# An expert's two vectors fetched by two indirect transfers instead of one

## The chip, the cores and the metric

The kernel runs on one core of one Trainium2 chip. The metric is the device time of one execution in microseconds (us). A core has TensorE (PE, matmuls), VectorE (DVE), ScalarE (ACT), GpSimd (POOL) and SyncE (SP), which run their own instruction streams and meet at semaphores, and 16 DMA engines that all queues share. SP and ACT issue plain transfers; GpSimd issues the indirect ones, which fetch rows named by indices in on-chip memory.

## The reference, cut to what matters

Two transformer blocks over 256 tokens of width 1024, in fp32. The second block has two layers, and each ends in a layer of "product key" experts: every token picks, for each of 8 heads, 16 of 16,384 experts, each a pair of vectors `u` and `v` of 1024 numbers.

```python
def peer_ffn(x, w_q, sub_keys, u, v):
    ...
        top_s, pos = lax.top_k(cand_s, PEER_TOPK)
        eidx = jnp.take_along_axis(cand_i, pos, axis=-1)
        gate = jax.nn.softmax(top_s, axis=-1).astype(xb.dtype)
        h = jax.nn.gelu(jnp.einsum('thkd,td->thk', u[eidx], xb), approximate=False)
        return jnp.einsum('thk,thkd->td', gate * h, v[eidx])
```

So for 2 layers x 256 tokens x 8 heads x 16 experts, two rows of 4 KB must be read: 536.9 MB in all. `u` is needed for a dot product with the token; `v` only afterwards, when the weight `gate * h` is known.

## The kernel before

The work of a layer's experts is cut in 16 units (2 groups of 128 tokens x 8 heads), each of 16 slots. A slot is one expert for each of 128 tokens, one token per partition. There are 256 slots per layer, 512 in all. The fetched vectors lie in `G`, a ring of `RING` = 8 slots with 2 x 1024 fp32 per partition. The first 1024 columns hold `u` and the last 1024 hold `v`, because the host has laid the two tables side by side (`uv0`, `uv1`: rows of 8 KB). A slot goes through five steps, each on its own engine:

1. GpSimd (L801 to L815) waits for `slot_free`, for the first slot of a unit also for `idx_ready`, and issues one indirect transfer of 128 rows of 8 KB into the slot, by the indices in a column of `EIDX`. It signals `gathered[slot]`. In the tables of the trace this is `arena<-uv,expert_index`.
2. VectorE (`slot_dots`, L1481 to L1486) waits for `gathered` and makes the dot product of `u` with the token.
3. ACT (`slot_weights`, L1015 to L1024) makes a diagonal matrix from gelu of the dot product (L1020), times the gate (L1023), and signals `diag_ready`.
4. TensorE (`weigh_slot`, L640 to L647) waits for `diag_ready` and multiplies the diagonal with `v`, in two matmuls of 512 columns that add up in PSUM over all slots. In the profile each is two records.
5. The second matmul signals `slot_free`, which lets GpSimd fill the slot again.

Beside the dot products VectorE picks the next units' experts: `piece` cuts the top-16 search of a unit into 16 pieces, one after each slot's dot product. TensorE, during the first 128 tokens of a layer, computes later heads' queries between the slots (`query_step`, L655) from weights that SP's queue streams in blocks of 1 MB (`w_ring`, L362). During the second 128 tokens no weights come. At the end of the first 128 tokens' work, their output norm (`output_norm`) runs on VectorE in the midst of the last unit, after its ninth slot. Then come the norm of the other tokens and the next layer; at the very end the output is stored by SP (L373), 128 rows of 4 KB for each group of tokens.

Of the kernel before, what the change touches and what calls it, by code (L numbers as in the profile page):

```python
# [176 lines left out]
        c.leave(times)  # L177


def build(nc, stream, keys, cols, rows, x_cm, p_cm, sgu_wt, rcnt_in, positions, decay, uv0, uv1, out):  # L180
    ctx = ExitStack()
    with ctx:
        def sb(name, shape, dt=FP32):
# [2 lines left out]
        def sem(name):  # L186
            return ctx.enter_context(nc.semaphore(name))
# [149 lines left out]
        idx_ready = sem("idx_ready")  # L337
        top_ready = sem("top_ready")
        exp_ready = sem("exp_ready")
        gathered = [sem(f"gathered{i}") for i in range(RING)]  # L340
        slot_free = sem("slot_free")
        dots_ready, gates_ready, diag_ready = sem("dots_ready"), sem("gates_ready"), sem("diag_ready")
        experts_summed = sem("experts_summed")
# [34 lines left out]
        def _(pe):  # L378
# [258 lines left out]
                ring.wait_stored(ring.n - 1)  # L637
                key_scores(2)

            def weigh_slot(tt, s, count):  # L640

                pe.wait_ge(diag_ready, count)
                slot = s % RING
                for c in range(2):
                    last = nc.tensor.matmul(AUX[2 * tt + c][:, :], DG[:, slot, :],  # L645
                                            G[:, slot, D + c * 512:D + (c + 1) * 512], start=False, stop=False)
                last.then_inc(slot_free, 1)  # L647

            def query_step(s):

# [16 lines left out]
            def experts(layer):  # L667
                base = layer * (PEER_SLOTS + 1) + 1
                for u in range(HEADS):
                    for s in range(TOPK):  # L670
                        weigh_slot(0, s, base + u * TOPK + s + 1)
                        if 1 <= u <= HEADS - AHEAD and s == 2:

                            ring.wait_stored(ring.n - 1)
                            key_scores(u + AHEAD - 1)
                        if u < HEADS - AHEAD:

                            for k in range(3) if u and s == 2 else () if u and s < 2 else (s,):
                                query_step(k)
                end_tokens(0)  # L680
                with pe.Fori(0, HEADS) as i:
                    for s in range(TOPK):
                        weigh_slot(1, s, base + HEADS * TOPK + s + 1 + i * TOPK)
                end_tokens(1)

            peer(0)
# [71 lines left out]
        @block.gpsimd  # L758
        def _(pool):
            chain = Chain(pool, pool_chain)  # L760
            link = chain.link
            nc.gpsimd.memset(ONES[:, :], 1.0).then_inc(ones_ready, 1)
            nc.gpsimd.memset(PADH[:, :, 0:PAD], 0.0)
            nc.gpsimd.memset(PADZ[:, :, 0:ZPAD], 0.0).then_inc(pads_ready, 1)
            link(nc.gpsimd.memset(IDENT[:, :], 1.0))
            link(nc.gpsimd.affine_select(out=IDENT[:, :], in_=IDENT[:, :], pattern=[[-1, P]],
                                         compare_op=ALU.is_equal, fill=0.0, base=0, channel_multiplier=1))
            nc.gpsimd.memset(ZERO[:, :], 0.0)
            link(nc.gpsimd.memset(ALPHA_I[:, :], ALPHA))
            nc.gpsimd.affine_select(out=ALPHA_I[:, :], in_=ALPHA_I[:, :], pattern=[[-1, P]],  # L770
                                    compare_op=ALU.is_equal, fill=0.0, base=0,
                                    channel_multiplier=1).then_inc(ident_ready, 1)
            link(nc.gpsimd.iota(IOTAI[:, :], pattern=[[1, TOPK]], base=0, channel_multiplier=0))
            link(nc.gpsimd.tensor_copy(IOTA16[:, :], IOTAI[:, :]))
            pool.sem_inc(iota_ready, 1)

            pool.wait_ge(sgu_w_loaded, 16)
            link(nc.gpsimd.memset(WS[P // 2:P, :, 0:P // 2], 0.0))
            pool.sem_inc(sgu_w_ready, 1)

            pool.wait_ge(small_loaded, 16)
            for u in range(8, 12):
                pool.wait_ge(acc_free[u % BANKS], u // BANKS + 1)
            for g in range(len(WINDOWS)):
                src, lo = PADZ[:, 2 * g:2 * g + 2, :], 0
                for n in range(g + 1):
                    dst, step = (PA, PB)[n % 2], 2 ** n
                    lo += step
                    link(nc.gpsimd.tensor_tensor(dst[:, :, lo:ZPAD + S], src[:, :, lo:ZPAD + S],
                                                 src[:, :, lo - step:ZPAD + S - step], ALU.add))  # L790
                    src = dst
                link(nc.gpsimd.tensor_tensor(POOLED[:, 2 * g:2 * g + 2, :], src[:, :, ZPAD:ZPAD + S],
                                             RC[:, g:g + 1, :].broadcast_to([P, 2, S]), ALU.mult))
                last = nc.gpsimd.tensor_tensor(POOLED[:, 2 * g:2 * g + 2, :], POOLED[:, 2 * g:2 * g + 2, :],
                                               PADZ[:, 2 * g:2 * g + 2, ZPAD:ZPAD + S], ALU.subtract)
                link(last) if g < 3 else last.then_inc(pooled_ready, 1)

            pool.wait_ge(input_ready, 10)
            nc.gpsimd.iota(DIFI, pattern=[[-P, 2], [1, S]], base=0, channel_multiplier=-1).then_inc(iota_ready, 1)  # L799

            for layer in range(2):  # L801
                uv = (uv0, uv1)[layer]
                free0 = layer * (RING + PEER_SLOTS)
                with pool.Fori(0, UNITS // 2) as i:
                    for par in range(2):
                        for s in range(TOPK):
                            n = par * TOPK + s
                            pool.wait_ge(slot_free, free0 + n + 1 + i * 2 * TOPK)
                            if s == 0:
                                pool.wait_ge(idx_ready, layer * UNITS + par + 1 + i * 2)  # L810
                            pool.sem_inc(waits_passed, 1)
                            pool.indirect_dma_start(  # L812
                                G[:, s % RING, :], None, uv,
                                bass.IndirectOffsetOnAxis(ap=EIDX[:, par, s:s + 1], axis=0),
                            ).then_inc(gathered[s % RING], 16)  # L815


        @block.scalar
# [285 lines left out]
        def _(dve):  # L1104
# [279 lines left out]
            def peer(layer):  # L1384
# [96 lines left out]
                def slot_dots(tt, unit, s, i):  # L1481
                    slot, n = s % RING, n0 + unit * TOPK + s
                    landed = 16 * (n // RING + 1)
                    dve.wait_ge(gathered[slot], landed if i is None else landed + i * 16 * (2 * TOPK // RING))
                    v.scalar_tensor_tensor(G[:, slot, 0:D], G[:, slot, 0:D], 1.0, HTM[:, tt, :], ALU.mult, ALU.mult,  # L1485
                                           accum_out=HD[:, slot:slot + 1]).then_inc(dots_ready, 1)  # L1486

# [123 lines left out]
def _layout(inputs):  # L1611
# [68 lines left out]
    def cm(a):  # L1680
# [8 lines left out]
        "sgu_wt": f("w_sgu_s")[0].transpose(2, 0, 1),  # L1689
        "rcnt": np.stack([1.0 / np.minimum(t1, np.float32(w)) for w in WINDOWS]).astype(np.float32),  # L1690
        "positions": f("positions_2")[0], "decay": f("ret_log1m_decay_2")[0].reshape(-1),
        "uv0": np.concatenate([f("peer_u_2")[0], f("peer_v_2")[0]], axis=1),
        "uv1": np.concatenate([f("peer_u_2")[1], f("peer_v_2")[1]], axis=1),
    }


# [12 lines left out]
```

## Time and profile before

| | |
|---|---|
| time, median of 3 runs | 2521.17 us (2519.57 to 2522.03) |
| the profiled execution | 2519.95 us, its span 2518.0 us |
| TensorE busy | 2187.0 us, 87% |
| VectorE busy | 1204.9 us, 48% |
| ACT busy | 687.8 us, 27% |
| GpSimd busy | 587.4 us, 23% |
| DMA | 701.47 MB, 279 GB/s over the span |
| of it the software queue (GpSimd's) | 536.90 MB, 51.3% of the engines' time |

The span is the time from the first to the last instruction of the profiled execution. Busy shares are means over the whole span, in which stages with different limits follow each other. The page therefore also cuts the span in 40 slices of 63 us, with each engine's busy tenths and the rate of the DMA engines in each. A "share of 16 engines" for a DMA queue is the sum of the times that its packets took, over 16 times the stretch asked for; packets may overlap a little, so it can exceed 100%.

### The profile page before, as it was taken

The numbers are of one execution on the slowest core, as the hardware profiler recorded it, in microseconds if no ns is written. First come the engines' busy times: TensorE is split into PE (matmuls) and PEld (weight loads), VectorE is DVE, ScalarE is ACT, GpSimd is POOL, SyncE is SP. The second block draws the span as 40 slices with busy tenths as digits, with TensorE's granted clock in tenths as the row PEclk, the third lists the DMA queues.
The fourth block names the chain that finished last, engine by engine and source line by source line (L and its number), as shares of the span: only waits on it lengthen the run. The fifth ranks groups of instructions, "written<-read, shape, count | busy, mean of one in ns | idle before, by whom it ended". The sixth has DMA issues, their size and how long they took to land.

```text
span 2518.0 us, 23594 instructions
## 1 busy us (share of the span) xinstructions
PE 2187.0 (87%) x7202; PEld 1339.6 (53%) x7202; DVE 1204.9 (48%) x2852; ACT 687.8 (27%) x1472; POOL 587.4 (23%) x546
## 2 busy tenths in 40 slices
PE   7989998999999997999878777778788997878786
PEld 6858887888775785444322222256654442322222
DVE  3972112000240204666666766522256666666665
ACT  1001101000201103343434344322234343434433
POOL 0300000000000001344444444400023444444441
PEclk9999998999999998999999999989999999999998
DMA  5433432444343234999999999921179999999997
GB/s 216 151 117 137 148 142 100 154 144 145 134 150 134 100 134 194 421 421 422 422 422 421 422 422 422 422 91 67 69 313 421 422 422 421 422 421 422 422 422 292
DMA packets 96981, 701.47 MB, mean 279 GB/s; under 512 B 10896, under 2 KB 11152, under 8 KB 11792
## 3 DMA queue, kind: packets, MB, share of 16 engines
q0 software_dynamic: 73728, 536.90, 51.3%
q1 hardware_dynamic: 21600, 156.25, 17.3%
q10 hardware_dynamic: 1584, 7.41, 0.8%
q8 instruction: 42, 0.69, 0.1%
q14 instruction: 27, 0.22, 0.0%
HBM read 699.47 MB, written 1.05 MB: 278 GB/s over the span
## 4 chain that ended last, share of the span: by engine, by line
PE 47%; DMA 34%; issue 7%; DVE 6%; ACT 4%; DVEq 1%; POOL 0%; POOLq 0%; ACTq 0%
DMA arena<-uv,expert_index 34%; PE acc L407 31%; PE aux L645 8%; PE acc L435 2%; DVE arena L1170 2%; PE aux L469 1%; ACT arena L1020 1%; ACT arena L1023 1%; DVE arena L1485 1%; PE acc L655 1%; PE aux L488 1%; DVE rstd L1124 0%; PE acc L599 0%; DVEq L106 0%; PE aux L634 0%
## 5 line engine op out<-in xcount | busy, mean ns | idle before, releaser
L645 PE MATMUL aux<-arena 128*128 128x512 f32 x2048 | 1015.2, 625 | 215.9 <-ACT arena L1023 210.2
L812 POOL DMA_INDIRECT arena<-uv,expert_index x512 | 561.7, 1097 | 1238.5 <-PE aux L645 670.5
L1485 DVE SCALAR_TENSOR_TENSOR arena<-arena 128x1024 f32<-128x1024 f32 x512 | 635.1, 1241 | 439.5 <-DMA arena<-uv,expert_index 439.5
L645 PEld LDWEIGHTS aux<-arena 128*128 128x128 f32 x2048 | 364.3, 193 | 791.8 <-ACT arena L1023 506.3
L407 PE MATMUL acc<-x,w_ring 128*128 128x256 f32 x2544 | 564.5, 385 | 27.7 <-issue 12.3
L407 PEld LDWEIGHTS acc<-x,w_ring 128*128 128x128 f32 x2544 | 491.2, 193 | 100.5 <-issue 23.5
L1020 ACT ACTIVATE arena<-ident,dots 128x128 f32<-128x128 f32 x512 | 205.3, 401 | 740.9 <-DVE arena L1485 739.3
L407 PE MATMUL acc<-arena,w_ring 128*128 128x256 f32 x1416 | 312.8, 383 | 13.5 <-DVEq L1551 7.0
L407 PEld LDWEIGHTS acc<-arena,w_ring 128*128 128x128 f32 x1416 | 271.1, 192 | 53.4 <-DVEq L1551 7.4
L1023 ACT ACTIVATE arena<-arena,gate 128x128 f32<-128x128 f32 x512 | 205.4, 401 | 17.0
L799 POOL IOTA arena<- 128x512 int32 x1 | 0.6, 558 | 556.4 <-DVEq L1281 556.4
L1170 DVE SCALAR_TENSOR_TENSOR arena<-arena,channel_vectors x240 | 112.2, 548 | 0.2 <-DVE arena L1170 0.2
L833 ACT ACTIVATE arena<-acc 128x512 f32<-128x512 f32 (+1 forms) x65 | 38.5, 595 | 250.2 <-PE acc L407 248.1
L655 PEld LDWEIGHTS acc<-x,w_ring 128*128 128x128 f32 x320 | 60.8, 192 | 67.0 <-issue 66.2
L655 PE MATMUL acc<-x,w_ring 128*128 128x256 f32 x320 | 93.5, 382 | 0.0
L435 PE MATMUL acc<-w_ring,x 128*128 128x512 f32 x192 | 82.7, 592 | 0.0
L1262 DVE TENSOR_TENSOR arena<-acc,arena 128x256 f32 x20 | 8.5, 425 | 131.7 <-ACT arena L921 131.7
L435 PEld LDWEIGHTS acc<-w_ring,x 128*128 128x128 f32 x192 | 36.5, 190 | 45.1 <-issue 45.0
L911 ACT ACTIVATE scratch<-arena 128x512 f32<-128x512 f32 x8 | 5.0, 629 | 189.2 <-DVE arena L1238 189.2
L1238 DVE COPY arena<-acc 128x512 f32<-128x512 f32 x8 | 5.5, 692 | 103.9 <-PE acc L407 103.9
L1129 DVE TENSOR_SCALAR rstd<-aux 128x256 f32<-128x256 f32 x9 | 3.8, 425 | 95.9 <-PE aux L469 92.1
L469 PE MATMUL aux<-scratch,ones 128*128 128x256 f32 x90 | 28.7, 488 | 22.3 <-ACT scratch L850 12.4
(209 smaller groups left out, 1079.4 us busy)
## 6 DMA issues: line engine op xcount, KB each, us to landing
w_ring<-stream SPq DMA_DIRECT2D x147, 1024.0 KB, 4.7
arena<-uv,expert_index POOLq DMA_INDIRECT x512, 14.9
x<-keys ACTq DMA_DIRECT2D x2, 1024.0 KB, 4.7
row_vectors<-rows ACTq DMA_DIRECT2D x2, 1024.0 KB, 8.1
row_vectors<-rows ACTq DMA_DIRECT2D x1, 1536.0 KB, 11.8
x<-x_cm SPq DMA_DIRECT2D x1, 1024.0 KB, 5.6
out<-arena SPq DMA_DIRECT2D x2, 512.0 KB, 5.1
arena<-rcnt ACTq DMA_DIRECT2D x1, 512.0 KB, 15.3
```

Source lines behind the costliest of these rows:

```text
L407: last = nc.tensor.matmul(ring.bank()[:, half * S:(half + 1) * S], w[:, 0, :], x[:, k, :], start=(k == 0), stop=(k == kt - 1))
L435: last = nc.tensor.matmul(bank[:, :], x[:, k, tt * P:(tt + 1) * P], w, start=(k == 0), stop=(k == kt - 1))
L469: last = nc.tensor.matmul(AUX[3 - half][:, 0:S], ONES[:, :], x[:, k, :], start=(k == 0), stop=(k == kt - 1))
L488: last = nc.tensor.matmul(AUX[3][:, 0:S], ONES[:, :], src[:, k, :], start=(k == 0), stop=(k == KT - 1))
L645: last = nc.tensor.matmul(AUX[2 * tt + c][:, :], DG[:, slot, :], G[:, slot, D + c * 512:D + (c + 1) * 512], start=False, stop=False)
L655: last = nc.tensor.matmul(ring.bank()[:, half * S:(half + 1) * S], w[:, 0, :], X0[:, k, :], start=(k == 0), stop=(k == KT - 1))
L812: pool.indirect_dma_start(G[:, s % RING, :], None, uv, bass.IndirectOffsetOnAxis(ap=EIDX[:, par, s:s + 1], axis=0),).then_inc(gathered[s % ...
L833: ring.release(nc.scalar.activation(dst, halves(ring.bank()), func, scale=scale))
L1020: link(nc.scalar.activation(DG[:, slot, :], IDENT[:, :], ACT.Gelu, scale=HD[:, slot:slot + 1]))
L1023: nc.scalar.activation(DG[:, slot, :], DG[:, slot, :], ACT.Copy, scale=GT[:, par, s:s + 1]).then_inc(diag_ready, 1)
L1170: chain.step(v.scalar_tensor_tensor(CV[:, j + c, :], at, w, CV[:, j + c, :], ALU.mult, ALU.add))
L1485: v.scalar_tensor_tensor(G[:, slot, 0:D], G[:, slot, 0:D], 1.0, HTM[:, tt, :], ALU.mult, ALU.mult, accum_out=HD[:, slot:slot + 1]).then_in ...
```

## The change

Each slot gets two indirect transfers, each of 128 rows of 4 KB. The first brings `u` into the slot's first half and signals `down_landed[slot]`, the second brings `v` into its second half and signals `up_landed[slot]`. The tables are four arrays instead of two. VectorE waits for the first signal alone. TensorE gets a wait for the second, ahead of the one for `diag_ready`. GpSimd's waits stay once per slot. The ring, the order of slots and the computation stay as they are.

```diff
-        gathered = [sem(f"gathered{i}") for i in range(RING)]
+
+        down_landed = [sem(f"down_landed{i}") for i in range(RING)]
+        up_landed = [sem(f"up_landed{i}") for i in range(RING)]
...
-            def weigh_slot(tt, s, count):
-
+            def weigh_slot(tt, s, count, landed):
+
+                pe.wait_ge(up_landed[s % RING], landed)
                 pe.wait_ge(diag_ready, count)
...
+            def landed(layer, unit, s):
+
+                return 16 * ((layer * PEER_SLOTS + unit * TOPK + s) // RING + 1)
...
-                uv = (uv0, uv1)[layer]
+                downs, ups = ((u0, v0), (u1, v1))[layer]
...
                             pool.indirect_dma_start(
-                                G[:, s % RING, :], None, uv,
+                                G[:, s % RING, 0:D], None, downs,
                                 bass.IndirectOffsetOnAxis(ap=EIDX[:, par, s:s + 1], axis=0),
-                            ).then_inc(gathered[s % RING], 16)
+                            ).then_inc(down_landed[s % RING], 16)
+                            pool.indirect_dma_start(
+                                G[:, s % RING, D:2 * D], None, ups,
+                                bass.IndirectOffsetOnAxis(ap=EIDX[:, par, s:s + 1], axis=0),
+                            ).then_inc(up_landed[s % RING], 16)
...
-                    dve.wait_ge(gathered[slot], landed if i is None else landed + i * 16 * (2 * TOPK // RING))
+                    dve.wait_ge(down_landed[slot], landed if i is None else landed + i * 16 * (2 * TOPK // RING))
...
-        "uv0": np.concatenate([f("peer_u_2")[0], f("peer_v_2")[0]], axis=1),
-        "uv1": np.concatenate([f("peer_u_2")[1], f("peer_v_2")[1]], axis=1),
+        "u0": f("peer_u_2")[0], "v0": f("peer_v_2")[0], "u1": f("peer_u_2")[1], "v1": f("peer_v_2")[1],
```

## Rows read from the trace of the kernel before

**Rows 1.** The page, the span in 40 slices: busy tenths, and GB/s of the DMA.

```profile
PE   7989998999999997999878777778788997878786
DVE  3972112000240204666666766522256666666665
POOL 0300000000000001344444444400023444444441
DMA  5433432444343234999999999921179999999997
GB/s 216 151 117 137 148 142 100 154 144 145 134 150 134 100 134 194 421 421 422 422 422 421 422 422 422 422 91 67 69 313 421 422 422 421 422 421 422 422 422 292
```

**Rows 2.** The page, the chain that ended last, shares of the span by engine.

```profile
PE 47%; DMA 34%; issue 7%; DVE 6%; ACT 4%; DVEq 1%; POOL 0%; POOLq 0%; ACTq 0%
```

**Rows 3.** DMA view, 1400 to 1500 us: packets, and the software queue (packets, MB, share).

```profile
DMA packets 5794, 42.21 MB, mean 422 GB/s; under 512 B 642, under 2 KB 642, under 8 KB 642
...
q0 software_dynamic: 5794, 42.21, 101.4%
```

**Rows 4.** The gather's line, L812, over the span.

```profile
L812 POOL DMA_INDIRECT arena<-uv,expert_index x512: 935/939/1994, 985.7 to 2484.6; - x171
...
DMA to landing us min/median/max: 5.6/14.9/19.4
```

**Rows 5.** Timeline, 1501 to 1514 us: start, us, engine, line, operation, [idle before].

```profile
1501.00 0.94 POOL L812 DMA_INDIRECT arena<-uv,expert_index  x1 [1.55 <-PE aux L645]
1501.01 1.25 DVE L1485 SCALAR_TENSOR_TENSOR arena<-arena 128x1024 f32<-128x1024 f32 x1 [1.00 <-DMA arena<-uv,expert_index]
...
1502.30 0.40 ACT L1020 ACTIVATE arena<-ident,dots 128x128 f32<-128x128 f32 x1 [1.65 <-DVE arena L1485]
1502.73 0.40 ACT L1023 ACTIVATE arena<-arena,gate 128x128 f32<-128x128 f32 x1
...
1503.19 1.98 PE L645 MATMUL aux<-arena 128*128 128x512 f32 x4 [0.50 <-ACT arena L1023]
...
1510.95 1.23 DVE L1485 SCALAR_TENSOR_TENSOR arena<-arena 128x1024 f32<-128x1024 f32 x1 [0.69 <-DMA arena<-uv,expert_index]
1511.04 1.96 POOL L812 DMA_INDIRECT arena<-uv,expert_index  x1 [1.62 <-PE aux L645]
```

**Rows 6.** DMA view, 2506 to 2518 us: the last store, alone on the engines.

```profile
DMA packets 144, 0.52 MB, mean 44 GB/s; under 512 B 16, under 2 KB 16, under 8 KB 144
...
q1 hardware_dynamic: 144, 0.52, 10.8%
...
out<-arena SPq DMA_DIRECT2D x1, 512.0 KB, 2.6
```

**Rows 7.** DMA view, 1700 to 1712 us: a weight load, SP's queue.

```profile
q1 hardware_dynamic: 144, 1.05, 25.4%
```

**Rows 8.** The page, DMA issues: operation, count, KB each, median us to landing.

```profile
w_ring<-stream SPq DMA_DIRECT2D x147, 1024.0 KB, 4.7
```

**Rows 9.** Timeline, 985 to 990 us: GpSimd's first issues, and SP's of weights.

```profile
987.11 0.33 SPq L362 DMA_DIRECT2D w_ring<-stream  x1
987.19 0.94 POOL L812 DMA_INDIRECT arena<-uv,expert_index  x1 [0.30 <-issue]
...
988.44 0.94 POOL L812 DMA_INDIRECT arena<-uv,expert_index  x1 [0.30 <-issue]
```

**Rows 10.** Timeline of GpSimd, 112 to 140 us: two instructions, a wait between.

```profile
111.30 1.33 POOL L792 TENSOR_TENSOR arena<-arena 128x512 f32<-128x512 f32 x1
112.71 1.33 POOL L794 TENSOR_TENSOR arena<-arena 128x512 f32<-128x512 f32 x1
```

**Rows 11.** The page, costliest groups: busy us, mean ns, idle before by releaser.

```profile
L812 POOL DMA_INDIRECT arena<-uv,expert_index x512 | 561.7, 1097 | 1238.5 <-PE aux L645 670.5
L1485 DVE SCALAR_TENSOR_TENSOR arena<-arena 128x1024 f32<-128x1024 f32 x512 | 635.1, 1241 | 439.5 <-DMA arena<-uv,expert_index 439.5
```

**Rows 12.** Timeline, 2487 to 2508 us: VectorE's norm of the first tokens, TensorE's last slots.

```profile
2488.86 1.22 DVE L1516 TENSOR_TENSOR arena<-arena,row_vectors 128x1024 f32<-128x1024 f32 x1
...
2492.16 14.78 PE L645 MATMUL aux<-arena 128*128 128x512 f32 x28 [5.83 <-ACT arena L1023]
```

**Rows 13.** DMA view, weights' queue: 987 to 1320 us, and 1848 to 2180 us.

```profile
q1 hardware_dynamic: 864, 6.29, 4.5%
...
q1 hardware_dynamic: 432, 3.15, 2.3%
```

More of the change, by code:

```diff
@@ L177, in repeat, with build @@
         c.leave(times)
-def build(nc, stream, keys, cols, rows, x_cm, p_cm, sgu_wt, rcnt_in, positions, decay, uv0, uv1, out):
+def build(nc, stream, keys, cols, rows, x_cm, p_cm, sgu_wt, rcnt_in, positions, decay, u0, v0, u1, v1, out):
     ctx = ExitStack()
@@ L670, in experts @@
                     for s in range(TOPK):
-                        weigh_slot(0, s, base + u * TOPK + s + 1)
+                        weigh_slot(0, s, base + u * TOPK + s + 1, landed(layer, u, s))
                         if 1 <= u <= HEADS - AHEAD and s == 2:
@@ L682, in experts @@
                     for s in range(TOPK):
-                        weigh_slot(1, s, base + HEADS * TOPK + s + 1 + i * TOPK)
+                        weigh_slot(1, s, base + HEADS * TOPK + s + 1 + i * TOPK,
+                                   landed(layer, HEADS, s) + i * 16 * (TOPK // RING))
                 end_tokens(1)
@@ L1706 @@
     build(nc, ap["stream"], ap["keys"], ap["cols"], ap["rows"], ap["x_cm"], ap["p_cm"], ap["sgu_wt"], ap["rcnt"],
-          ap["positions"], ap["decay"], ap["uv0"], ap["uv1"], out)
+          ap["positions"], ap["decay"], ap["u0"], ap["v0"], ap["u1"], ap["v1"], out)
     return run(nc, [arrays], core_ids=[0]).results[0]["out"]
```

## The prediction

> **What bounds the kernel now.** I read the page's slices first. In the two stretches where the experts are gathered (slices 17 to 26 and 31 to 39) the 16 DMA engines are busy 9 tenths or more of the time and move 421 to 422 GB/s in nearly every slice, while TensorE, VectorE and GpSimd have slack [rows 1]. Outside them no gather runs, so the change can act only inside. The chain of waits puts 34% of the span on one transfer, `arena<-uv,expert_index` [rows 2]. Next the queue by itself, in 100 us without other traffic: 5794 packets, of which 144 make a transfer (128 rows of 8 KB, and 16 small ones that signal), so 40.24 transfers in 100 us: a period of 2.485 us for one expert slot of 128 tokens, at a busy share of 101.4% [rows 3]. The reader is to see that a share of 100% with a flat rate is a full pipe. The issues confirm it: median 14.9 us from issue to landing, minimum 5.6 [rows 4], so 9 us of queue stand in front of each gather. The ring of 8 slots closes the loop: 8 x 2.485 = 19.9 us, of which 14.9 are queue and transfer and 5.0 are dot product, diagonal, matmul and re-issue. From this I take it that a shorter reaction by any compute engine buys nothing there; only a cheaper or dearer transfer does, or an issuer that can't keep up.
>
> One slot in the timeline shows the other engines: dot product 1.25 us, ACT 0.40 + 0.40, matmuls 1.98, all inside the period of 2.49 [rows 5].
>
> **The change, part by part.**
>
> *DMA.* 512 gathers of 128 x 8 KB become 1024 of 128 x 4 KB: the same bytes, twice the packets. Now a slot takes 101.4% x 16 x 100 us / 40.24 = 40.3 us of engine time [rows 3]. The trace has no 4 KB gather. It has one transfer of that form alone on the engines, the last store, 128 rows of 4 KB: 144 packets, 10.8% of 16 x 12 us = 20.7 us [rows 6]. Two make 41.5 us, 1.029 times 40.3. The period grows to 2.485 x 1.029 = 2.556 us, +0.071; times 512 slots that is **+36.4 us**. Nothing hides it, because the engines are full [rows 1]. Bounds: below, nothing, since a lone weight load of 1 MB, also 8 KB rows, needed 25.4% x 16 x 12 = 48.8 us [rows 7], more than the two stores together, so packet size is not the only thing that prices a transfer. Above, by landing times: a 4 KB-row transfer lands after 2.6 us, an 8 KB-row one after 4.7 us [rows 6, 8]; two of the first cost 0.5 us more than one of the second, and were this shown in full, 512 slots would pay 256 us. But it is latency, and 9 us of queue lie over latency; I take +36, from the row that measures occupancy.
>
> The rows show 2.9% more for half the packet size, if a store stands for a gather. The Trainium skill (DMA: Bandwidth & Descriptors, Why small descriptors are slow) gives a fixed overhead of about 3 cycles a packet beside one cycle per 32 bytes; as an estimate from that page 262 cycles replace 259, 1.2%, and the sum would be about +15 us instead of +36. No row here separates the two.
>
> *GpSimd.* It issues twice per slot. An issue takes 0.94 us when nothing is in its way, and with all slots free the next follows 0.30 us later [rows 9]. The gap holds a wait and a counter, which the second issue of a slot lacks; two plain GpSimd instructions with a wait between them stand 0.08 us apart [rows 10]. So two issues cost 2 x 0.94 + 0.30 + (0.08 to 0.30) = 2.26 to 2.48 us, against 2.556 of DMA: just covered, by 0.08 to 0.30 us. Now the same engine has 1.24 us of work in 2.485 and nobody waits for it.
> There is a catch in the rows. When an issue begins inside a dot product on VectorE, it takes longer: begun 0.09 us after the dot product, it took 1.96 us and ended 0.8 us after the dot product's end; begun with it, 0.94 [rows 5]. The mean over 512 issues is 1.097 us [rows 11], 0.157 above the median of 0.939. Now most issues are released by TensorE at a point of the cycle just ahead of the dot product. With two per slot they can't both be there. I take the case that one waits for the dot product's end and the second fits behind it: 2.556 - 1.25 = 1.3 us are free of the dot product in each period, and two issue starts need 1.02 to 1.24 us between them. Then GpSimd follows the DMA's pace and costs nothing.
> The Trainium skill (SBUF — State Buffer, Who interferes with whom) says that a VectorE instruction with two SBUF inputs contends with a GpSimd instruction that reads SBUF, and that the later one waits; the 1.96 us row agrees. It speaks against this change, and the second and third case below are what it would do.
>
> *VectorE* waits for the first half alone, about 1.28 us sooner. Under a full queue that only moves its idle time: the 439.5 us of waiting [rows 11] are a wait for bytes. *TensorE* gets one wait more per slot, on the second half. That half lands about 1.28 us after the first, while the diagonal is ready only 1.25 + 0.1 + 0.85 = 2.2 us after it [rows 5]: satisfied 0.9 us before TensorE looks. Behind it in TensorE's queue stand the next slot's matmuls and query steps, and GpSimd waits for their release; if the cover were gone, the ring's queue time would still take up to 9 us. The instruction itself lies in TensorE's gap of 0.5 us per slot [rows 5]. *The ends*: at each layer's end TensorE works off a backlog of seven slots (28 matmuls in 14.8 us), since VectorE has spent the time before on the other tokens' norm [rows 12], so the earlier half saves between 0 and 1.28 us, twice; I take 0. *SP and ACT queues* keep their transfers; their 8 KB packets now stand beside 4 KB ones, which can only bring weights sooner. Tables in HBM keep their total size.
>
> **Sum.** 2519.95 us for the profiled execution (2518.0 span, 1.95 around it) + 36.4 = 2556.4. The median of the runs is 1.2 us above that execution: **2558 us**.
>
> **The rivals.**
>
> *GpSimd paces, one wait per slot* (chance 0.24). Gap 0.30 for both issues and the mean excess once per slot: 2 x 1.24 + 0.157 = 2.64 us per slot. It doesn't hold everywhere: in the first tokens' half of each layer weights share the engines, 4.5% of 333 us = 15.0 us in the first layer, 2.3% of 332 us = 7.6 in the second [rows 13]. Per half of 128 slots GpSimd needs 337.9 us, DMA 128 x 2.556 = 327.2 plus weights. Layer 1's first half is then DMA's, +9.1 us; layer 2's first half 337.9 - (318.1 + 7.6) = +12.2; the two second halves 337.9 - 318.1 = +19.8 each. Sum +60.9: 2582 us. For it: the gap of 0.30 is the only one measured between issues. Against: weights and jitter let it catch up.
>
> *GpSimd and VectorE in lock step* (0.12). Without a queue a half lands about 5.6 - 1.24 = 4.4 us after its issue, its dot product ends at 5.6, and the issue two slots later, due at 2 x 2.48 = 4.96, waits for that end: two slots per 5.6 us, 2.8 each. The mean issue gives nearly the same, 2 x (1.097 + 0.30) = 2.79. By halves as before: +24.5, +31.9 and twice +39.5, in all +135: 2656 us. For it: the start, where issues at 1.24 us and halves at 1.28 us build no queue. Against: a weight load of 2.5 us pushes the halves back and builds one, and one stands at 987.11, at the start of the gathers [rows 9].
>
> *Not slower* (0.08). Halves cost the engines no more per byte, which [rows 7] permit, and GpSimd keeps up; then the period stays 2.485 and the ends save up to 2 x 1.28: 2519 us. It decides where a slot's extra falls below 5.0 / 512 = 0.01 us. To be faster by over 0.2% it would need a rate above the flat 422 GB/s as well.
>
> *Forecast: the DMA engines pace* (0.50), own range 2539 to 2575: half to one and a half times the +36. *Something beyond these* (0.06): sixteen transfers in flight instead of eight, which no row shows, stop the issuer: above 2660.
>
> **Numbers.** This kernel's measurement tells about 0.2%, 5 us. Slower: 0.92 (the forecast, both GpSimd cases, the last). Within: 0.05, faster 0.03, both from the third rival. The range goes from 2539, below which only the third rival lies, to 2660, which takes in the lock step.
>
> **What the profile after would show.** Packets of the software queue double to 147,456 with the same bytes. If I am right, the gather stretches keep a busy share near 100% at about 410 GB/s (421 x 2.485 / 2.556), both halves of a layer grow alike (+9.1 us each), VectorE still waits for DMA, and GpSimd's issues number 1024 with idle time between them that TensorE ends. If GpSimd paces, the share falls to 95% or less in the second halves, landing times drop from 14.9 towards 5 us, GpSimd's idle time is "issue" alone, and its mean issue is over 1.1 us. What would make the forecast wrong first is the gap between a slot's two issues, then the share of issues that meet a dot product, then the price of a 4 KB read.

## The result and the profile after

The changed kernel takes 2720.45 us (median of 4 runs, 2714.16 to 2729.37), the kernel before took 2520.72 beside it: ratio 1.0795, interval [1.0759, 1.0831], about +200 us. The forecast was 2558, the range ended at 2660. The profiled execution took 2724.96 us with a span of 2723.1.

From the page after: DMA busy share and GB/s in 40 slices, the software queue, the chain by engine, and the three groups that answer to [rows 2, 11].

```profile
DMA  5433424443432369999999999621599999999997
GB/s 215 145 118 139 141 107 146 149 152 134 146 139 93 124 251 370 379 369 376 341 369 354 351 364 367 239 94 62 202 367 353 341 350 358 368 359 361 355 355 300
q0 software_dynamic: 147456, 536.94, 52.7%
PE 49%; issue 22%; POOL 10%; DMA 7%; DVE 5%; ACT 3%; another core or an unknown queue 3%; DVEq 1%; POOLq 0%; ACTq 0%
L1497 DVE SCALAR_TENSOR_TENSOR arena<-arena 128x1024 f32<-128x1024 f32 x512 | 627.0, 1226 | 617.0 <-DMA arena<-u,expert_index 544.7
L824 POOL DMA_INDIRECT arena<-v,expert_index x512 | 584.0, 1141 | 157.6 <-issue 150.2
L820 POOL DMA_INDIRECT arena<-u,expert_index x512 | 523.3, 1022 | 752.1 <-DVE expert_index L1480 505.1
```

Packets doubled at the same bytes, as the change says. But where before moved a flat 421 to 422 GB/s [rows 1], after moves 341 to 379, uneven from slice to slice, and the gather fell from 34% of the chain [rows 2] to 7%. DMA engines still read 9 tenths: the digit alone would hide the loss, the rate shows it. The engines are no longer a full pipe.

Where the time went: from the start of a layer's first issue to the end of its last, the gathers run from 987.05 to 1737.8 and from 1942.5 to 2703.7 us (before: 985.7 to 1629.6 and 1849.3 to 2485.6). Divided by 256 slots, a slot takes 2.93 and 2.97 us; before it took 2.515 and 2.486. That is +106.9 and +124.9 us. The stretch from the first layer's last issue to the second layer's first shrank by 15.0 us (219.7 to 204.7) and that from the last issue to the span's end by 13.0 (32.4 to 19.4), presumably because no queue is left to drain; the start is 1.4 later. In all +205.2, the difference of the spans (205.1).

GpSimd by itself explains 2.76 us of the 2.95: 1.022 and 1.141 us for the two issues, and twice a gap of 0.30 us. The remaining 0.18 us per slot are pauses: 35 gaps between issues exceed 1 us, and what they have over 0.30 us comes to 93 us in all; the longest are 4.4 us and, once, 10.5. Next the waits between 1000 and 1700 us, within layer 1's gathers, after: us in total, times, longest.

```profile
PEld aux L648 <- issue: 335.6, 639, 10.8
DVE arena L1497 <- DMA arena<-u,expert_index: 261.0, 198, 4.6
ACT arena L1032 <- issue: 231.8, 121, 5.7
ACT arena L1032 <- DVE arena L1497: 180.4, 87, 4.9
...
POOL arena L820 <- PE aux L648: 28.9, 16, 4.4
...
DVE top_pairs L1448 <- remote: 1.5, 1, 1.5
```

and the same view of the kernel before, 1000 to 1600 us, three of its eleven rows:

```profile
ACT arena L1020 <- DVE arena L1485: 343.6, 208, 4.1
POOL arena L812 <- PE aux L645: 325.6, 191, 5.8
...
PEld aux L645 <- issue: 127.0, 510, 0.5
```

Two things are new. Engines are idle for up to 10.8 us with the releaser "issue", that is, with nothing in the profile left to wait for; before, the longest such wait was 0.5 us at the same line. And VectorE waits for signals of its own chain (briefly here, the last row of the first table; for 2.17 us in a timeline below).

So the signals can be timed directly, by pairing each producer's end with its consumer's start and counting only the time in which the consumer had nothing else to do. For the activation on ACT that waits for the k-th dot product, that is its start, less the dot product's end or the end of ACT's operation before it, whichever is later. Before, none of the 512 starts is over 0.3 us late by this count; after, 16 are, the latest by 6.3 us. For GpSimd, it is the start of a slot's first issue, less the end of the matmul that frees the slot or the end of GpSimd's instruction before, over the 466 slots that wait for neither new indices nor the first fill of the ring. Before, 4 starts come over 1 us late; after, 30, the latest by 4.4 us. What those over 0.5 us have above the usual gap of 0.30 us comes to some 80 us, against the 93 us of pauses. (The ends of matmuls are modelled in the profile, so a tenth of a microsecond counts for nothing here.) So most of the pauses is time in which TensorE has already freed the slot and GpSimd doesn't know it. Signals between engines arrive late.

Few transfers are under way meanwhile. Each transfer ends with 16 packets of 4 bytes, which in order give its landing: after, half of the transfers land within 5.6 us of their issue (14.9 before [rows 4]), and when GpSimd issues, 3 are in flight in the median and never more than 6.

### The profile page after: what moved, and what is told of

Read it like the earlier page. It is cut to its first block, busy times and chain, and to the rows that moved or that the text cites. A ratio compares the mean times of both kernels' runs of the same rounds, so it can differ in the third digit from the quotient of the medians.

```text
span 2723.1 us, 24394 instructions
## 1 busy us (share of the span) xinstructions
PE 2201.6 (81%) x7202; PEld 1351.5 (50%) x7202; DVE 1195.8 (44%) x2852; ACT 688.5 (25%) x1472; POOL 1133.1 (42%) x1058
## 4 chain that ended last, share of the span: by engine, by line
PE 49%; issue 22%; POOL 10%; DMA 7%; DVE 5%; ACT 3%; another core or an unknown queue 3%; DVEq 1%; POOLq 0%; ACTq 0%
PE acc L409 28%; PE aux L648 13%; POOL arena L824 5%; POOL arena L820 5%; DMA arena<-u,expert_index 4%; DMA arena<-v,expert_index 3%; PE acc L437 2%; DVE arena L1182 2%; PE aux L471 1%; PE acc L662 1%; ACT arena L1035 1%; ACT arena L1032 1%; PE aux L490 0%; DVE rstd L1136 0%
## 5 line engine op out<-in xcount | busy, mean ns | idle before, releaser
L648 PE MATMUL aux<-arena 128*128 128x512 f32 x2048 | 1034.6, 634 | 399.8 <-issue 187.6
L1497 DVE SCALAR_TENSOR_TENSOR arena<-arena 128x1024 f32<-128x1024 f32 x512 | 627.0, 1226 | 617.0 <-DMA arena<-u,expert_index 544.7
L648 PEld LDWEIGHTS aux<-arena 128*128 128x128 f32 x2048 | 373.9, 197 | 975.2 <-issue 741.0
L820 POOL DMA_INDIRECT arena<-u,expert_index x512 | 523.3, 1022 | 752.1 <-DVE expert_index L1480 505.1
L824 POOL DMA_INDIRECT arena<-v,expert_index x512 | 584.0, 1141 | 157.6 <-issue 150.2
```

The lines of the kernel that those rows point to most:

```text
L820: pool.indirect_dma_start(G[:, s % RING, 0:D], None, downs, bass.IndirectOffsetOnAxis(ap=EIDX[:, par, s:s + 1], axis=0),).then_inc(down_la ...
L824: pool.indirect_dma_start(G[:, s % RING, D:2 * D], None, ups, bass.IndirectOffsetOnAxis(ap=EIDX[:, par, s:s + 1], axis=0),).then_inc(up_la ...
```

## The experiments

### Whose wait is it? Dot product, TensorE's new wait

**one_input_dot**: the dot product becomes a sum of one operand, the rest as changed. **one_input_dot_before**: the same in the kernel before.

```diff
-v.scalar_tensor_tensor(G[:, slot, 0:D], G[:, slot, 0:D], 1.0, HTM[:, tt, :], ALU.mult, ALU.mult,
-                       accum_out=HD[:, slot:slot + 1]).then_inc(dots_ready, 1)
+v.tensor_scalar(G[:, slot, 0:D], G[:, slot, 0:D], 1.0, 0.0, ALU.mult, ALU.add,
+                accum_out=HD[:, slot:slot + 1]).then_inc(dots_ready, 1)
```

> The changed kernel, but VectorE's dot product reads one operand from SBUF instead of two: it sums u alone, the product with the token is left out, so the expert weights are others. Theory 1 (GpSimd issues twice per slot, and the issues that begin inside a two-operand dot product wait for its end): the wait is gone, every issue takes 0.94 us, the mean of both lines is below 1.0 us, a slot costs GpSimd 2.48 us and the DMA engines' 2.556 us pace: 2560 us; up to 2650 if the pauses of 2 to 4 us that GpSimd makes about every 15 slots stay. Theory 2 (packets of 4 KB cost the DMA engines more than the store showed, GpSimd is only near its limit by chance): unchanged, 2720 us.

> The kernel before with the same one-operand sum instead of the dot product (the product with the token is left out). Both theories: the DMA engines pace here with or without the waits of GpSimd, so 2520 us within 10; only the mean issue falls from 1.10 to 0.94 us.

Measured: 2720.32 us (two executions, ratio 1.0793 [1.0762, 1.0824]); in the kernel before 2519.27 against 2519.63, one execution. The issues did fall to 0.947 and 0.942 us: their excess came from the dot product's second operand. But no time came back. Three quarters of the slots now take at most 2.49 us, GpSimd's 2 x (0.30 + 0.945), and pauses fill the rest, 228 us in place of 93. Here is one, from the timeline (start us, length, engine, in brackets the idle time before):

```profile
1502.05 0.08 DVE L1497 DVE_READ_ACCUMULATOR arena<-arena 128x1 f32 x1
...
1504.60 0.08 DVE L1497 DVE_READ_ACCUMULATOR arena<-arena 128x1 f32 x1
1505.34 0.40 ACT L1032 ACTIVATE arena<-ident,dots 128x128 f32<-128x128 f32 x1 [4.90 <-DVE arena L1497]
1505.44 0.94 POOL L824 DMA_INDIRECT arena<-v,expert_index  x1 [0.30 <-issue]
...
1506.63 0.41 DVE L1445 MATCH_REPLACE8 arena<-top_pairs,arena 128x256 f32<-128x256 f32 x1
1506.95 1.21 DVE L1497 TENSOR_SCALAR_CACHE_REDUCE arena<-arena 128x1024 f32<-128x1024 f32 x1
1508.13 0.08 DVE L1497 DVE_READ_ACCUMULATOR arena<-arena 128x1 f32 x1
1509.55 0.40 ACT L1032 ACTIVATE arena<-ident,dots 128x128 f32<-128x128 f32 x1 [3.38 <-DVE arena L1497]
...
1510.31 0.94 POOL L820 DMA_INDIRECT arena<-u,expert_index  x1 [3.94 <-PE aux L648]
1510.39 0.43 DVE L1448 MAX8 top_pairs<-arena 128x8 f32<-128x256 f32 x1 [2.17 <-remote]
```

The dot products that end at 1502.13 and 1504.69 are answered by ACT at 1505.34 and 1509.55, after 3.2 and 3.4 us in which ACT is idle (before the second it still had the first one's work until 1506.17); the three ahead of them were answered after 0.04. VectorE's operation of 1506.63 ends at 1507.04, the dot product behind it at 1508.21, and the next operation of its own chain begins at 1510.39; nothing but the chain's signal lies between. GpSimd's pause of 3.94 us begins and ends among these: it is one victim among four engines. By the counts above, 49 of ACT's starts are over 0.3 us late here and 54 of GpSimd's over 1 us.

**both_waits_on_dve**: TensorE's new wait removed, VectorE waits for both halves.

```diff
-                pe.wait_ge(up_landed[s % RING], landed)
...
-                    dve.wait_ge(down_landed[slot], ...)
+                    for arrived in (down_landed, up_landed):
+                        dve.wait_ge(arrived[slot], ...)
```

> The changed kernel without TensorE's new wait: VectorE waits for both halves before the dot product. If TensorE's wait holds back its releases of slots (theory C, for the pauses in which GpSimd gets no release for 2 to 4 us and then several at once), the pauses go and the time falls to 2640 us or below. If not, 2720 us, since about 1.3 us of longer reaction per slot lie under the ring's 8 slots.

Measured: 2716.09 us (one execution), 2.93 and 2.93 us per slot. That lies within the spread of the changed kernel, so neither TensorE's wait nor VectorE's earlier start shows any worth.

### The packet price alone

**plain_second**: u gathered as changed, v as a plain transfer of 128 rows of 4 KB from ACT's queue, six slots ahead (always the first 128 rows of the table, so it isn't the experts' vectors).

```diff
-                            pool.indirect_dma_start(
-                                G[:, s % RING, D:2 * D], None, ups, ...
+                act.wait_ge(slot_free, ...)
+                act.dma_start(G[:, n % RING, D:2 * D], ups[0:P, :]).then_inc(up_landed[n % RING], 16)
```

> u comes by GpSimd's gather of 128 rows of 4 KB; v comes by a plain transfer of 128 rows of 4 KB that ACT issues six slots ahead (always the first 128 rows of the table, so the values are not those of the chosen experts). The packets are those of the changed kernel, GpSimd issues once. Theory 1: the DMA engines pace at 2.556 us per slot, 2560 us, or a little more where ACT's issues delay its own work. Theory 2: 2720 us, since the packets are the same.

Measured: 2557.27 us (two executions, 2557.23 and 2557.32), ratio 1.0146 [1.0117, 1.0176], +37.6 us; GB/s in 40 slices:

```profile
GB/s 215 155 115 141 140 140 106 156 148 148 121 156 136 83 115 287 409 410 410 409 410 409 410 410 409 396 66 66 115 321 410 409 409 409 409 409 409 410 410 281
```

This is the forecast, 2558 us and 410 GB/s, obtained with one GpSimd issue per slot.

**halves_by_tokens**: the table of before, two gathers of 64 rows of 8 KB into 64 partitions each, the same indices for both.

```diff
+                            for h, landed in ((0, gathered), (1, gathered2)):
+                                lo = h * (P // 2)
+                                pool.indirect_dma_start(
+                                    G[lo:lo + P // 2, s % RING, :], None, uv,
+                                    bass.IndirectOffsetOnAxis(ap=EIDX[0:P // 2, par, s:s + 1], axis=0),
```

> The kernel before, its one gather of 128 rows of 8 KB cut into two of 64 rows (tokens 0 to 63, tokens 64 to 127) with their own signals; VectorE waits for both. The second gather uses the indices of the first 64 tokens, so half of the tokens get others' experts. Two issues per slot, but together only as many rows and packets of 8 KB as before. Theory A (a slot with two software transfers is held at about 2.95 us, 1.47 us per transfer, whatever they carry): 2720 us. Theory B (the limit is on rows, that is descriptors, about 10 ns each): 2520 to 2540 us. Waits of issues for VectorE's dot product alone would give at most 2.76 us per slot, 2640 us.

Measured: 3422.02 us (one execution). Both theories missed: once the gathers are under way the DMA engines read 9 tenths busy at 226 to 311 GB/s, landing takes 29.1 us in the median, and GpSimd waits for TensorE. A gather into 64 partitions costs the DMA engines more per byte: a packet of 8 KB took 0.50 us between 1400 and 1500 us, against 0.31 before. As a test of the number of issues it is void; why a 64-row gather is slow wasn't followed up.

### The number of transfers

**small_second**: before's gather of 8 KB rows, and a second one of 128 rows of 64 bytes into a tile of its own. **small_second_16**: 16 such rows. **three_issues**: two such gathers beside the large one. **second_on_odd**: one, in odd slots only.

```diff
-                                G[:, s % RING, 0:D], None, downs,
+                                G[:, s % RING, :], None, downs,
...
-                                G[:, s % RING, D:2 * D], None, ups,
+                                TINY[:, s % RING, :], None, ups,
```

> One gather of 128 rows of 8 KB per slot as before, and a second one of 128 rows of 64 bytes into a tile that nobody reads; waits as in the changed kernel. Two issues per slot, but the vectors come in 8 KB packets. Theory 1: nearly as slow as the changed kernel, 2.76 to 2.95 us per slot: 2650 to 2720 us. Theory 2: the large packets carry it, 2525 to 2550 us.

> As the run with a small second gather (128 rows of 8 KB, then rows of 64 bytes), but the second has 16 rows instead of 128. Theory A (per transfer): 2720 us. Theory B (per row): 144 rows instead of 256, the DMA engines pace, 2520 to 2545 us; and the issue of 16 rows would take clearly less than 0.94 us.

> 128 rows of 8 KB and twice 128 rows of 64 bytes per slot: three issues. Issue time alone (3 x 1.24 = 3.73 us per slot) gives 2520 + 512 x 1.24 = 3155 us. Theory A or B (1.47 us per transfer of 128 rows): 4.4 us per slot, about 3510 us.

> The before kernel's gather of 8 KB rows for every slot, and a second gather of 128 rows of 64 bytes into a tile of its own in the odd slots only: three GpSimd transfers for two slots. Every result is computed. Theory A (a GpSimd transfer costs 1.47 us of some limit, whatever its size): 1.5 x 1.47 = 2.20 us per slot, below the 2.485 of the DMA engines, so 2520 to 2530 us (the small packets' DMA time, at most 10 us). Theory B (the pauses come from two issues standing back to back, so each pair brings its share): half of the 0.18 to 0.25 us of pauses per slot comes back at every second slot and the queue covers most of it; 2530 to 2620. If the loss were simply by the number of added transfers, half of +200: 2620.

Measured: small_second 2721.53 us (two executions, ratio 1.0798 [1.0763, 1.0833]), 2.98 and 2.92 us per slot; small_second_16 2711.94 (one execution), 2.91 and 2.94; three_issues 3418.39 (one execution), 4.31 and 4.31; second_on_odd 2537.81 (2535.66 to 2538.82; ratio 1.0067 [1.0051, 1.0084]), at a flat 417 GB/s. The three groups of three_issues:

```profile
L832 POOL DMA_INDIRECT tiny<-t,expert_index x512 | 574.0, 1121 | 158.0 <-issue 152.7
L828 POOL DMA_INDIRECT tiny<-t,expert_index x512 | 570.4, 1114 | 156.1 <-issue 153.1
L824 POOL DMA_INDIRECT arena<-uv,expert_index x512 | 496.8, 970 | 758.2 <-DVE expert_index L1488 506.0
```

Here GpSimd's own time is 0.970 + 1.114 + 1.121 + 3 x 0.30 = 4.10 us, the slot 4.31 (the forecast of the per-transfer theory was 4.4). As the second of two, a gather of 1 KB costs as much as one of 512 KB: 2.91 to 2.98 us for two, 4.31 for three, 1.44 to 1.49 each. With 1.5 per slot the limit, 2.2 us, lies under the DMA engines' 2.485, and only the added transfers' DMA time is left: 17.2 us over 256 transfers, 0.067 us each, more than the 10 us in all that theory A allowed.

### Bytes, spacing, depth

**half_the_bytes**: the changed kernel, with 64-byte rows for v; TensorE weighs u's rows. **half_the_bytes_one_input**: with the sum of one operand too.

```diff
-                                            G[:, slot, D + c * 512:D + (c + 1) * 512], start=False, stop=False)
+                                            G[:, slot, c * 512:(c + 1) * 512], start=False, stop=False)
```

> The changed kernel with the second gather cut to 64 bytes per row into a tile of its own; TensorE weighs the first half's rows instead. Half of each expert's data is left out, so the DMA engines carry half the bytes. Theory A (the limit is by transfer and owes nothing to the bytes): 2.93 to 2.97 us per slot as before, 2710 to 2725 us. Theory B (the pauses and the late signals come from DMA engines that are nearly full): the pauses go, and GpSimd's own 2 x (0.30 + about 1.06) = 2.72 us per slot remain: 2720 - 512 x 0.23 = about 2600 us.

> The same with the sum of one operand instead of the dot product. Theory A: 2710 to 2725 us again. Theory B: GpSimd's own time alone, 2 x (0.30 + 0.945) = 2.49 us per slot: 2720 - 512 x 0.46 = about 2485 us.

Measured: 2700.64 us (ratio 1.0722 [1.0704, 1.0740]) and 2693.01 (1.0692 [1.0674, 1.0710]); 2.90 and 2.90, 2.88 and 2.90 us per slot, at some 185 GB/s. That is 9 to 17 us below what theory A allowed and far from theory B: half the bytes are worth 20 to 27 us of the 200. Full DMA engines aren't the cause. The queue of half_the_bytes from 1400 to 1500 us, packets, MB and share of the engines' time:

```profile
DMA packets 6201, 18.70 MB, mean 187 GB/s; under 512 B 1138, under 2 KB 1708, under 8 KB 6200
...
q0 software_dynamic: 6200, 18.70, 64.7%
```

**padded_one_input**, **padded_192**, **padded_384**: one_input_dot with a fill of 64, 192 or 384 columns by GpSimd ahead of every issue.

```diff
+                            pool.wait_ge(filled, ...)
+                            pool.sem_inc(waits_passed, 1)
+                            nc.gpsimd.memset(FILLER[:, :], 0.0).then_inc(filled, 1)
                             pool.indirect_dma_start(
```

> The changed kernel with the sum of one operand instead of the dot product (there GpSimd issued for 2 x 1.245 us and paused for 0.45 us per slot), and with a small fill of a tile by GpSimd ahead of every issue, which spaces the issues by some 0.1 to 0.3 us more. Theory A (a limit of about 1.47 us per transfer; the pauses are only where it shows): the fills come out of the pauses, 2715 to 2735 us as long as an issue with its fill and gaps stays below 1.47 us, and the pauses shrink from 228 us by what the fills take. Rival (each issue, or each transfer, brings its share of pauses whatever the spacing): the fills add in full, 1024 x 0.1 to 0.3 = +100 to +300 us, 2820 to 3020.

> The kernel with a fill ahead of every issue, the fill three times as wide (estimate from 0.167 us for 64 columns: about 0.30 us). An issue with its fill then takes about 1.41 us in place of 1.28, 2.82 per slot. Theory M (limit of 1.45 per transfer): 2.93 to 2.97 us per slot, 2725 to 2750 us, with pauses down from 0.43 to about 0.1 us per slot. Additive pauses: 2.98 + 0.27 = 3.25 us per slot, about 2880 us.

> The fill six times as wide (estimate 0.50 us). An issue with its fill takes about 1.61 us, 3.22 per slot. Theory M: the issuer's own time is now the longer, no pauses, 3.22 us per slot, about 2870 us. Additive pauses: 2.98 + 0.66 = 3.64 us per slot, about 3085 us.

From the timeline of padded_384:

```profile
1504.78 0.43 POOL L832 MEMSET filler<- 128x384 f32 x1
1505.37 0.95 POOL L833 DMA_INDIRECT arena<-v,expert_index  x1 [0.16 <-POOL filler L832]
1506.32 0.43 POOL L825 MEMSET filler<- 128x384 f32 x1
1506.92 0.95 POOL L826 DMA_INDIRECT arena<-u,expert_index  x1 [0.16 <-POOL filler L825]
```

| kernel | us | slot, median | slot, mean | the rest |
|---|---|---|---|---|
| one_input_dot | 2720.32 | 2.48 | 2.946 | 0.46 |
| padded_one_input | 2744.60 | 2.55 | 2.979 | 0.43 |
| padded_192 | 2731.34 | 2.77 | 2.967 | 0.20 |
| padded_384 | 2835.32 | 3.09 | 3.173 | 0.08 |

(us per slot; the median is GpSimd's own pace, since at least half of the slots have no pause.) The first fill lay mostly within the gap of 0.30 us and tested little: 36 us more of own time, 24 us more in all, between the two theories. The second is decisive: 0.22 us more of own time per slot than the first and 13 us less in all. The pauses gave way. With the third GpSimd is the pace, the pauses are nearly gone, and the time is below the 2870 expected, since the fill took 0.43 us and not 0.50. Additive pauses would have given 2880 and 3085.

The late signals go in steps. Of GpSimd's starts 54 came over 1 us late in one_input_dot; with the three fills it is 43, 17 and 0. Of ACT's starts 49 came over 0.3 us late; with the fills 1, 0 and 0. So the first fill, 0.03 us per issue, all but ended the lateness between VectorE and ACT, while the slot stayed at 2.98 us: those late signals accompany the limit and don't make it.

**ring_of_16_one_input**, **ring_of_16**: the half-byte kernels with 16 slots of 4 KB.

```diff
-RING = 8
+RING = 16
-        G = region(0, RING, 2 * D)
+        G = region(0, RING, D)
-        DG = region(109, RING, P)
+        DG = sb("diagonals", [P, RING, P])
```

> The kernel with half the bytes per slot and the sum of one operand, with a ring of 16 slots of 4 KB in place of 8. Theory L (release signals reach GpSimd late by up to some 10 us, and eight slots, 20 us, less the 10 us that a slot needs from issue to release, don't cover it): sixteen slots, 40 us, cover it, the pauses go, and GpSimd's own 2 x 1.245 = 2.49 us per slot remain: 2693 - 512 x 0.40 = about 2490 us. Theory M (a limit of about 1.45 us per GpSimd transfer): the ring changes nothing, 2685 to 2700 us, and the pauses stand where they stood.

> The same ring of 16 with the dot product kept. Theory L: GpSimd's own time, 2 x 0.30 + 1.154 + 1.016 = 2.77 us per slot in place of 2.90: 2701 - 512 x 0.13 = about 2633 us. Theory M: 2695 to 2705 us.

Measured: 2693.26 us (ratio 1.0704 [1.0672, 1.0735]) and 2717.65 (1.0785 [1.0754, 1.0816]). Depth gives nothing; theory L, a bounded lateness that slots can cover, fell. The second is 17 us slower than half_the_bytes and 13 above what theory M allowed; why is open, and differences of that size between these kernels carry no argument. What depth does is let the signals fall further behind: of ACT's starts 107 are over 0.3 us late in place of 53 with the one operand, the latest by 9.0 us in place of 7.4, and 65 in place of 22 with the dot product, the latest by 7.6 in place of 4.1.

### Indirect or any?

**plain_small_second**: small_second with a plain second transfer from GpSimd's own queue.

```diff
-                            pool.indirect_dma_start(
-                                TINY[:, s % RING, :], None, ups,
-                                bass.IndirectOffsetOnAxis(ap=EIDX[:, par, s:s + 1], axis=0),
-                            ).then_inc(up_landed[s % RING], 16)
+                            pool.dma_start(TINY[:, s % RING, :], ups[0:P, :]).then_inc(up_landed[s % RING], 16)
```

> The before kernel's gather of 8 KB rows for every slot, and as second transfer a plain one of 128 rows of 64 bytes from GpSimd's queue, without indices. Every result is computed. If the limit belongs to any transfer that GpSimd issues: 2.93 to 2.97 us per slot, 2710 to 2725 us. If it belongs to indirect transfers alone: the small packets' DMA time remains, twice what the kernel with a second gather in the odd slots showed, +17 x 2: about 2555 us.

Measured: 2556.87 us (2556.25 to 2558.78), ratio 1.0149 [1.0132, 1.0166]. GpSimd's timeline and the rates in 1400 to 1500 us:

```profile
1499.81 1.70 POOL L821 DMA_INDIRECT arena<-uv,expert_index  x1 [0.30 <-issue]
1501.50 0.58 POOL L825 DMA_DIRECT2D tiny<-t  x1
1502.38 1.70 POOL L821 DMA_INDIRECT arena<-uv,expert_index  x1 [0.30 <-issue]
```

```profile
DMA packets 6874, 41.27 MB, mean 413 GB/s; under 512 B 1251, under 2 KB 1876, under 8 KB 1876
```

A plain transfer takes GpSimd 0.58 us with no gap before it. Two transfers per slot in the same queue, with packets of the same number and sizes as in small_second, and 165 us less: the pipe is full again. What is limited is indirect transfers.

Two things in these rows need care. The indirect issue takes 1.70 us here (0.94 elsewhere), because it begins inside the dot product, and 1.70 + 0.58 + 0.30 = 2.58 us leave GpSimd no slack either. Yet the engines pace: from 1400 to 1500 us the queue's packets take 101.7% of their time, the gather still lands 15.0 us after its issue in the median, and up to 12 transfers are in flight, twice as many as in the changed kernel, without a pause of the kind above (none of ACT's starts is over 0.3 us late, none of GpSimd's over 1 us). And the profile records the small rows in packets of 512 bytes, 16 to a transfer, and 16 that signal: the added transfer has 32 packets and not 144.

## Why the prediction was wrong

**The DMA term had the right size, and in part by luck.** +0.071 us per slot, +36.4 in all, was read from one store; plain_second gave +37.6 (0.073). By the overhead that the Trainium skill gives (DMA: Bandwidth & Descriptors, Why small descriptors are slow) it would have been +15, as the prediction estimated; the measurement decides against it here. But the prediction's reason, that rows of half the size cost 2.9% more, isn't what the other runs show: plain_small_second leaves the 8 KB rows whole, adds 32 packets to a slot in place of 144, and pays +36.8 us (0.072 per transfer); second_on_odd pays 0.067 for the same 32. Of these the added 8 KB themselves are about 0.02 (an estimate, from before's 2.485 us for 1 MB). The rest, about 0.05, comes with a quarter of the packets that cost 0.073 in plain_second, so most of the price goes by the added transfer and little by the number of its packets or the size of its rows. That a lone store, which holds no second transfer, showed the same figure is luck as far as these runs tell.

**The step that failed** is that two issues cost GpSimd 2.26 to 2.48 us and are "just covered" by the DMA engines' 2.556, so that GpSimd "costs nothing". Three terms of it:
- The gap before a slot's second issue was set between 0.08 and 0.30. It is 0.30: the wait and the counter don't make it, since the second issue lacks them. A fill of 0.17 us fits almost wholly into it (issue to issue 1.28 us in place of 1.245), so it belongs to the indirect issue. The 0.08 came from two instructions of another kind [rows 10], and no row showed two issues without a counter between.
- The contention was sized at one wait per slot or none; the measured means, 1.022 and 1.141, make 2.76 us with the gaps, near the lock step's 2.79. So GpSimd's own time alone was already 0.20 us over the 2.556 that were to cover it. But this term wasn't what set the time: one_input_dot took 0.27 us per slot out of it and 0 us came back.
- What set it, no view of before shows: with two or three per slot, indirect transfers came at one per 1.43 to 1.50 us over a layer and in no run faster, with half of the bytes or all, 16 rows or 128, and whatever GpSimd's own time below that (2.49 us for two in one_input_dot, 2.76 in the changed kernel). Two per slot took at least 2.87 us, against 2.485. Before had one in 2.485 and was far from it.

**The rivals.** One wait per slot (2582) and lock step (2656) both name GpSimd, which is the right engine, and the wait for the dot product as the cause. That wait is real, but one_input_dot took it away and the time stayed. The time fell into "something beyond these", above 2660, which had 0.06. Its mechanism as written, sixteen transfers in flight that stop the issuer, isn't borne out: at most 6 were in flight in the changed kernel when GpSimd issued, and plain_small_second had up to 12 without the loss.

**What held.** TensorE's wait and VectorE's earlier start were worth nothing (both_waits_on_dve). The ends were small, though they gave 13 to 15 us each and not 0 to 1.28, presumably since with GpSimd pacing there is no backlog to work off (not tested). The marks named for a pacing GpSimd held in part: the queue's share fell from 101.4% to 95.9% between 1400 and 1500 us (95% or less was named), landing fell to 5.6 us, the mean issue is over 1.1 us for one of the two, but GpSimd's idle time isn't "issue" alone, since late releases are in it.

**Open.** What carries the limit. Shown is that spacing the issues removes the pauses, that most of the pauses is time in which a released slot isn't yet seen, that a deeper ring lets lateness grow, and that signals among engines which have nothing to do with the gather are late in the same stretches. That the indirect issue and the engines' signals share a path which is served at about one issue per 1.45 us fits all of it, but is argued, not shown; nothing here looks into that path. The DMA engines are touched as well: in half_the_bytes, between 1400 and 1500 us, the queue's packets took 64.7% of the engines' time for 187 GB/s, while plain_second's two queues took 102.8% for 410; by the byte that is 1.4 times as much on engines with room to spare. Whether this is the same cause or a second effect no run tells. Half the bytes moved the limit by 0.05 us per slot, so traffic has at most a small part in it.

## What to carry to other kernels

Count GpSimd's indirect transfers against a rate, not only against their summed time: here one per 1.43 to 1.50 us was the most that a kernel sustained with two or three per slot, about the same whether the second brought 16 rows of 64 bytes or 128 rows of 4 KB, so fetch as much as possible per index and put what needs no indices on plain transfers. When an engine is idle with "issue" as the releaser for microseconds, and a deeper ring doesn't help, pair the producers' ends with the consumers' starts before looking for a data wait, and count only time in which the consumer was idle with nothing else ahead of it: an engine's backlog looks like a late signal otherwise. Test a suspected rate by adding spacing: if the time grows by less than the spacing, the pauses were the limit's own.

## What the runs showed of the hardware

- With two or three indirect gathers per slot, one took 1.43 to 1.50 us on the average of a layer, above the issuer's own 1.245 us (half_the_bytes_one_input, padded_one_input, three_issues); a plain transfer from the same queue takes the issuer 0.58 us and brings no such pauses (plain_small_second).
- Where the issuer's own time lies below that, signals between other engines came late in bursts: VectorE's to an idle ACT by up to 6.3 us (at most 0.1 before), and by up to 9.0 us with a ring of 16.
- One more transfer costs full DMA engines about 0.07 us (plain_small_second, second_on_odd, plain_second), though it brings 32 packets more in the first two and 144 in the third.
- An indirect issue of 0.94 us has a gap of 0.30 us ahead of it even without a wait; a fill of 0.17 us fits into it almost wholly (padded_one_input).
- Gathers of 64 rows into 64 partitions brought the engines, at 9 tenths busy, down to about 228 GB/s in most of the second layer (halves_by_tokens).
